# Building the keys and values of both heads of a pair before the attention of either, in a hybrid decoder layer on eight cores

## What is computed

```
q  = (rmsnorm(q_lat) @ w_uq).reshape(B, S, 16, 128 + 64)      # q_lat: 512 wide
kv = (rmsnorm(kv_lat) @ w_ukv).reshape(B, S, 16, 128 + 128)   # kv_lat: 256 wide
q_nope, q_pe = q[..., :128], q[..., 128:]
k_nope, v    = kv[..., :128], kv[..., 128:]
q_pe, k_pe   = apply_rope(q_pe), apply_rope(k_pe)             # k_pe is shared by the heads
s = (q . [k_nope, k_pe]) * 192 ** -0.5, causal
o = softmax(s) @ v
```

## Time and profile before

| | |
|---|---|
| median of 3 runs | 5439.72 us (5438.18 to 5873.62) |
| profiled execution | 5437.82 us, span 5436.2 us (5414.0 to 5436.2 on the cores) |
| PE busy | 4536.3 us, 83% |
| DVE busy | 1777.3 us, 33% |
| ACT busy | 1527.0 us, 28% |
| POOL busy | 208.3 us, 4% |
| mean granted clock of PE, profiled core | 0.921 |

### The profile page before, as it was taken

The page is one execution under the profiler, slowest core; times in us unless marked ns, Lnnn a source line. Parts: engine busy times, 40 slices in busy tenths (PEclk is TensorE's granted clock), DMA queues, the critical chain, the costliest instruction groups (busy, mean ns, idle before and its releaser), DMA issues.

```text
span 5436.2 us, 64110 instructions; the slowest of 8 cores (5414.0 to 5436.2 us)
## 1 busy us (share of the span) xinstructions
PE 4536.3 (83%) x23800; PEld 2196.8 (40%) x23800; DVE 1777.3 (33%) x2983; ACT 1527.0 (28%) x2567; POOL 208.3 (4%) x255
## 2 busy tenths in 40 slices
PE   0657988889966599788889973999999999994995
PEld 0323434444433244344444442444444444443443
DVE  0230015652122311244442115555555555002002
ACT  0441013330113410155451126444444443001001
POOL 1000000000000000000000000000000000110010
PEclk9978999889977799999999985999999999997997
DMA  9626634754455244110114446223232321996996
GB/s 152 124 33 89 93 61 70 115 81 72 77 147 125 35 74 74 33 24 13 19 20 67 75 116 194 50 57 60 51 66 51 66 51 53 219 219 181 218 217 181
DMA packets 354497, 505.64 MB, mean 93 GB/s; under 512 B 9232, under 2 KB 293904, under 8 KB 341648
## 3 DMA queue, kind: packets, MB, share of 16 engines
q0 software_dynamic: 267840, 282.08, 33.3%
q1 hardware_dynamic: 86352, 219.47, 12.7%
HBM read 726.96 MB, written 56.62 MB: 144 GB/s over the span
## 4 chain that ended last, share of the span: by engine, by line
PE 77%; DMA 8%; DVE 7%; ACT 3%; issue 2%; another core or an unknown queue 1%; DVEq 0%; POOL 0%; ACTq 0%; SPq 0%; POOLq 0%
PE ps L1031 22%; PE ps L1079 11%; PE ps L603 4%; PE ps L912 4%; PE ps L631 4%; PE ps L511 4%; PE ps L641 4%; PE ps L947 4%; PE ps L922 4%; DMA out<-sb_scr 3%; PE ps L883 2%; DMA wslot<-w_ada 2%; PE ps L869 2%; PE ps L871 2%; PE ps L885 2%
## 5 line engine op out<-in xcount | busy, mean ns | idle before, releaser
L1031 PE MATMUL ps<-sb_big,wslot 128*128 128x512 bf16 x5632 | 1217.7, 379 | 0.0
L1031 PEld LDWEIGHTS ps<-sb_big,wslot 128*128 128x128 bf16 x5632 | 551.6, 98 | 665.7 <-issue 2.5
L1044 DVE SCALAR_TENSOR_TENSOR sb_scr<-sb_scr,sb_cols 128x512 f32<-128x512 f32 x704 | 529.0, 751 | 469.2 <-ACT sb_scr L1040 431.4
L1079 PE MATMUL ps<-sb_mergedT,wslot 128*128 128x512 bf16 x2816 | 615.5, 382 | 46.2 <-DMA sb_mergedT<-gv_scr 29.2
L1079 PEld LDWEIGHTS ps<-sb_mergedT,wslot 128*128 128x128 bf16 x2816 | 276.5, 98 | 384.9 <-issue 58.4
L1038 ACT ACTIVATE sb_scr<-ps 128x512 f32<-128x512 f32 x352 | 210.2, 597 | 679.4 <-PE ps L1031 482.6
L878 ACT ACTIVATE sb_scr<-ps 128x512 bf16<-128x512 f32 (+3 forms) x640 | 333.8, 533 | 174.7 <-PE ps L871 87.9
L846 DVE RECIPROCAL sb_scr<-ps 128x512 f32<-128x512 f32 x64 | 214.9, 3358 | 389.8 <-PE ps L885 389.8
L1040 ACT ACTIVATE sb_scr<-ps,sb_cols 128x512 f32<-128x512 f32 x352 | 271.8, 772 | 0.0
L869 PE MATMUL ps<-sb_scr 128*128 128x512 bf16 (+3 forms) x640 | 231.0, 361 | 24.3 <-DVE sb_scr L826 21.5
L631 PE MATMUL ps<-sb_big,wslot 128*128 128x512 bf16 x1024 | 233.5, 381 | 16.8 <-DMA wslot<-w_ag 16.8
(11 more groups left out here) (158 smaller groups left out, 4038.5 us busy)
## 6 DMA issues: line engine op xcount, KB each, us to landing
sb_mergedT<-gv_scr SPq DMA_DIRECT2D x88, 1024.0 KB, 6.5
wslot<-w_ada POOLq DMA_DIRECT2D x24, 2048.0 KB, 23.8
wslot<-w_up POOLq DMA_DIRECT2D x22, 2048.0 KB, 14.6
wslot<-w_down POOLq DMA_DIRECT2D x88, 512.0 KB, 8.6
wslot<-w_in POOLq DMA_DIRECT2D x16, 2048.0 KB, 16.2
sb_scr<-x SPq DMA_DIRECT2D x32, 1024.0 KB, 6.7
wslot<-w_ag POOLq DMA_DIRECT2D x16, 2048.0 KB, 14.2
wslot<-w_bg POOLq DMA_DIRECT2D x16, 2048.0 KB, 14.1
```

Source lines behind the costliest of these rows:

```text
L1031: ins = e.matmul(ps[pb][:, :], lhsT=wv[:, kc, c0:c0 + 128], rhs=h2T[:, kc, tsl], start=(kc == 0), stop=(kc == KC - 1))
L1044: P.op("dve", lambda e, hb=hb, yb=yb, ch=ch, tap=tap, off=off: e.scalar_tensor_tensor(out=yb, in0=hb[:, off:off + 512], scalar=cols[:, C_C ...
L1079: ins = e.matmul(ps[oc * 2 + t2][:, :], lhsT=wv[:, f, oc * 128:(oc + 1) * 128], rhs=gslot[sl_][:, f, t2 * 512:(t2 + 1) * 512], start=(g == ...
```

## The change

The K/V projections of both heads are emitted before the score stage of either. For that the second head gets buffers of its own, `KnT_b` and `Vh_b`, with tokens of their own. They are not part of `scr`. The loop over `hd` is split in two, and the tuple `KV` says which buffers a head uses. The numbers of matmuls, copies, loads and bank allocations stay the same, and so does the order of the allocations from `pbank`.

```diff
+    KnT_b = sb("KnT_b", [128, S], BF16)
+    Vh_b = sb("Vh_b", [128, 16, 128], BF16)
...
+    t_KnT_b = P.toks(4)
+    t_Vh_b = P.tok()
+    KV = ((KnT, Vh, t_KnT, t_Vh), (KnT_b, Vh_b, t_KnT_b, t_Vh_b))
...
             for hd in range(2):
-                h = 2 * pr + hd
+                KnT_h, Vh_h, t_KnT_h, t_Vh_h = KV[hd]
                 for kt in range(nk512):
...
-                    P.op("dve", lambda e, pb=pb, ksl=ksl: e.tensor_copy(out=KnT[:, ksl], in_=ps[pb][:, :]),
-                         reads=[t_ps[pb]], writes=[t_KnT[kt]])
+                    P.op("dve", lambda e, pb=pb, ksl=ksl, KnT_h=KnT_h: e.tensor_copy(out=KnT_h[:, ksl], in_=ps[pb][:, :]),
+                         reads=[t_ps[pb]], writes=[t_KnT_h[kt]])
...
-                         reads=[t_ps[pb2]], writes=[t_Vh])
+                         reads=[t_ps[pb2]], writes=[t_Vh_h])
+            for hd in range(2):
+                h = 2 * pr + hd
+                KnT_h, Vh_h, t_KnT_h, t_Vh_h = KV[hd]
                 LOOK = 2
                 pend = []
...
-                    P.op("pe", f, reads=[t_Vh, t_pt[k_], t_ones], writes=[t_ps[po_], t_ps[psm_]])
+                    P.op("pe", f, reads=[t_Vh_h, t_pt[k_], t_ones], writes=[t_ps[po_], t_ps[psm_]])
...
-                            e.matmul(ps[pb][:, c0:512], lhsT=KnT[:, kb * 128:(kb + 1) * 128], rhs=QnT[hd][:, qsl],
+                            e.matmul(ps[pb][:, c0:512], lhsT=KnT_h[:, kb * 128:(kb + 1) * 128], rhs=QnT[hd][:, qsl],
...
-                        P.op("pe", mms, reads=[t_KnT[kb // 4], t_QnT[hd], t_Qr[hd], t_kpe[kb // 4], t_ident, t_mask],
+                        P.op("pe", mms, reads=[t_KnT_h[kb // 4], t_QnT[hd], t_Qr[hd], t_kpe[kb // 4], t_ident, t_mask],
                              writes=[t_ps[pb]])
...
-                            e.matmul(ps[po][:, c0:512], lhsT=Vh[:, kb, :], rhs=ptile[sl_][:, c0:512], start=(kb == 0),
+                            e.matmul(ps[po][:, c0:512], lhsT=Vh_h[:, kb, :], rhs=ptile[sl_][:, c0:512], start=(kb == 0),
                                      stop=(kb == nkb - 1))
```

More of the change, by code:

```diff
@@ L837, in attention @@
                     P.op("pe", mmv, reads=[wt, t_kvg[0][kt], t_kvg[1][kt]], writes=[t_ps[pb2]])
-                    P.op("act", lambda e, pb2=pb2, kt=kt: e.activation(out=Vh[:, 4 * kt:4 * kt + 4, :].rearrange("p k d -> p (k d)"),
+                    P.op("act", lambda e, pb2=pb2, kt=kt, Vh_h=Vh_h: e.activation(out=Vh_h[:, 4 * kt:4 * kt + 4, :].rearrange("p k d -> p (k d)"),
                                                                        in_=ps[pb2][:, :], func=AF.Copy),
-                         reads=[t_ps[pb2]], writes=[t_Vh])
+                         reads=[t_ps[pb2]], writes=[t_Vh_h])
+            for hd in range(2):
+                h = 2 * pr + hd
+                KnT_h, Vh_h, t_KnT_h, t_Vh_h = KV[hd]
                 LOOK = 2
@@ L848, in finalize, with emit_pend @@
                                                           op=ALU.mult), reads=[t_ps[po], t_rec], writes=[t_oT[h][tt]])
-                def emit_pend(ent):
+                def emit_pend(ent, t_Vh_h=t_Vh_h):
                     f, k_, po_, psm_, fin = ent
-                    P.op("pe", f, reads=[t_Vh, t_pt[k_], t_ones], writes=[t_ps[po_], t_ps[psm_]])
+                    P.op("pe", f, reads=[t_Vh_h, t_pt[k_], t_ones], writes=[t_ps[po_], t_ps[psm_]])
                     if fin is not None:
@@ L866, in attention, with mms @@
                         cnt += 1
-                        def mms(e, hd=hd, kb=kb, i=i, c0=c0, qsl=qsl, pb=pb):
-                            e.matmul(ps[pb][:, c0:512], lhsT=KnT[:, kb * 128:(kb + 1) * 128], rhs=QnT[hd][:, qsl],
+                        def mms(e, hd=hd, kb=kb, i=i, c0=c0, qsl=qsl, pb=pb, KnT_h=KnT_h):
+                            e.matmul(ps[pb][:, c0:512], lhsT=KnT_h[:, kb * 128:(kb + 1) * 128], rhs=QnT[hd][:, qsl],
                                      start=True, stop=False)
@@ L880, in attention, with mmo @@
                              reads=[t_ps[pb]], writes=[t_pt[sl_]])
-                        def mmo(e, kb=kb, c0=c0, sl_=sl_, nkb=nkb, po=po, psm=psm):
-                            e.matmul(ps[po][:, c0:512], lhsT=Vh[:, kb, :], rhs=ptile[sl_][:, c0:512], start=(kb == 0),
+                        def mmo(e, kb=kb, c0=c0, sl_=sl_, nkb=nkb, po=po, psm=psm, Vh_h=Vh_h):
+                            e.matmul(ps[po][:, c0:512], lhsT=Vh_h[:, kb, :], rhs=ptile[sl_][:, c0:512], start=(kb == 0),
                                      stop=(kb == nkb - 1))
```

## The result

The changed kernel takes 5350.95 us in the median. Set against runs of the kernel before on the same chips, the ratio is 0.983, with a 95% interval from 0.9816 to 0.9845: 1.7% faster. The cores of the profiled execution need 5312.8 to 5349.3 us, where they needed 5414.0 to 5436.2; their mean falls from 5422 to 5332.

A forecast was written before the change was run, and what follows sets the result against it. TensorE was taken as the bound, with 130 us idle and some low clock in attention. The terms -117.1 + 29.4 + 2.0 - 2.4 + 7.2 + 3.2 - 4.3 - 5.9 + 1.0 gave -86.9 us: 5352, range 5325 to 5400.

The forecast's parts named there:

- the bounds of the sum: Whole kernel with all unknowns at their dear or cheap ends: gain 56 us (time 5383) to 103 us (time 5336).
- within 2%: Whole kernel: time differs from before by no more than 2% (109 us); chance 0.84, against 0.14 faster and 0.02 slower.
- The removed stage: Middle K/V stage between the heads' scores leaves its place: 50.4 us in block 0, 66.8 in block 1, minus 117.1.
- Front, block 1: Before head 0's scores: head 1's K/V matmuls plus 29.4 us, later score start plus 2.0, K cast waits minus 2.4.
- Front, block 0: Before head 0's scores: head 1's K/V matmuls slip into existing waits; scores 0.9 us later per pair, plus 7.2.
- PV wait: Block 0, head 1's second PV half waits 0.4 us per pair for banks 1 and 4: plus 3.2 us.
- Clock in block 0: Score stages in block 0 regain clock as idle PE shrinks: minus 4.3 us for head 1, minus 5.9 for head 0.
- the second rival: Clock comes back whole, with front waits at 0.35 us and no wait of head 1's PV: 5338 us; chance 0.18.
- Loads: Block 0, pair 0: its successor's weights, loaded behind two `w_ada` loads, may land 0 to 2.8 us late; plus 1.0.
- The third rival: Block 0 becomes bound by loads: pairs 0 to 3 wait some 3 us each, 18 us in all, 5370; chance 0.06.
- move to the front: Rival in block 1: four added casts exposed before scores and PE at lower clock, 4.0 us a pair, 5385; chance 0.12.
- many short stops: Rival at head 0's scores: bank stops hold PE near clock 0.71, costing 89 us, 5441 or slower; chance 0.03.

The follow-up runs named there:

- the filling of the front wait: The kernel before, with 10 unused matmuls of 512 columns in front of head 0's scores in each pair of block 0; ratio 0.9977.
- the best kernel: The changed kernel with projection banks restarted at each pair as 2, 3, 5, 6, 7, 1, 4 and Q copies on ACT; 5297 us, mean over cores 5279.

## Why the prediction was right, and where it failed

**The time.** 5352 was forecast and 5351 measured, and the walk through the queues behind it holds nearly row by row. The step that failed is the last one, "Two per cent, about what a measurement of this kernel can tell from no change". The runs showed an interval of a seventh of a per cent to each side, so a gain of 1.7% is eleven times clear of no change. By that bound 0.84 was given to "within 2%" for a case whose own rows said faster in every branch but one: the bounds of the sum ended at 56 us of gain. The chances should have said that the kernel gets faster, and how sure that was. Two terms of the sum behind the time were mis-sized as well, the clock in block 0 and the loads, and hit it only together (below).

**The removed stage** (-117.1) is gone, with the idle time that hung on it.

**Front, block 1** (plus 29.4, 2.0 and minus 2.4). About 8.5 us from the first K matmul to the first score was stated. The front stages now take, in stretches of PE:

```profile
2400.31:2408.66 8.35, 7.18 (x81) 1.00 0.00 0
...
sum 66.03, PE 58.13; mean PE 7.27
```

Eight last 66.0 us, 8.3 each, with another 2.7 us of score waits in all. Block 1 gained 42.7 where the terms give 37.8. Part of the 4.9 us between them is in the Q stages (2.3 by my reading of the trace), where PE is busy for 2.4 us less; I had left them as they were.

**Front, block 0** (plus 7.2): the extra wait is 0.8 a pair by my reading of the trace, instead of 0.9. "About 4.5" for the stage was a slip of mine, since 1.9 + 2.2 + 0.9 is 5.0, and 5.1 is measured. **PV wait** (plus 3.2): 2.2 measured (L891 behind L855, eight times 0.3), so the place was right.

**Clock in block 0** (minus 10.2) was mis-sized: 20.7 us of busy time came back, of which 14.1 reached the length of the score stages, with the PV wait already in it; the two terms together had 7.0. I took half of head 0's loss because a shorter stop stayed. Every one of the eight pairs now has 1.00, and the filling of the front wait showed that all of head 0's loss hung on that one wait. What I had as the second rival is in this term the truth. I had also left out that PE at full clock waits more for ACT.

**Loads** (plus 1.0) were mis-sized the other way: 9.3 us on core 7, 7.9 on core 5, 4.8 on the mean. I read the landing time of 24.9 on the profiled core, in pair 3; in pairs 0 to 2 of that core the second block took 26.4, 25.6 and 26.7. On core 3 of the same execution the one of pair 0 took 34.5 us, which I hadn't looked at:

```profile
wslot<-w_ada POOLq DMA_DIRECT2D x1, 2048.0 KB, 34.5
```

The third rival, loads as bound, is thus true for pair 0 alone and small for the others. The clock is wrong by some 7 us one way and the loads by 8.3 on core 7 the other way, so they cancel on the slowest core. The 4.9 us more of block 1 are met by as much scatter outside attention: the stages lose 91.7 us from core 5 to core 7, the spans 86.9. That the sum (-86.9) equals the last number is luck; on the mean of the cores the stages gain 95. Of the signs stated, idle PE fell by 54 us where 60 to 75 were named, and the clock in block 0 is 0.94 where 0.91 to 0.93 was: less from idle time, more from the clock. The waits at the change of pair, whose growth would have proved the prediction wrong, did not grow (20.9 us against 20.7 in block 1).

**Rivals.** The wait didn't move to the front in block 1: no stage there exceeds 8.6 us. The wait at the meeting of the heads is gone. PE isn't slowed by many short stops: the projections have V waits of 1.2 us at most, and the clock behind them is 1.00. The Trainium skill, "TensorE: Matmul & The Clock Gate", "A second HAM failure mode: psum-queue depth-cycling", describes a PE that cycles through PSUM banks and stops so often between groups of matmuls that its clock swings. This trace doesn't bear that out: all 16 front stages, with twice the projections in a row, have 1.00.

**What stays open.** On core 5 the middle stages of three pairs in block 1 kept a clock of 1.00 behind idle times of 2.8 to 3.2 us, while others of 3.2 to 4.5 lost it. The length of the stop alone doesn't decide: on core 7 of the same execution the same 3.17 us gave 0.84 and 0.88 in two of those three pairs. Why is open. That the loads of all cores compete in pair 0 is argued from the spread between cores, and wasn't tried.

## What to carry to other kernels

Where an engine with an in-order queue idles at a seam, ask first which lock it stands at (here banks that a slow reciprocal still reads), and then which lock stands behind that (the queue of the engine that empties the banks); curing one gives its full worth only with the other. A second buffer is worth what it lets move: left in place it gave nothing, with the stage moved 95 us. Moving the stage was not the only cure: other banks and copies on ACT gave 112 us in the old order (5421.5 to 5310), and the best kernel, which has the new order as well, 145 (5424 to 5279). And look at the slowest core of each load before a transfer is called hidden, since the next stage may come to it on any core.

## What the runs showed of the hardware

- Idle stretches of 2.2 to 4.5 us cost TensorE another third to three quarters of their length through its clock (core 5): 13.9 us of busy time behind 19.1 us of waits in block 0 (head 0), 9.4 behind 28.1 in block 1. Filled with useless matmuls the same stages run at 1.00, and with the filling in block 1 the kernel with more work is the faster one (ratio 0.9976).
- In one execution of the kernel before, the same second load of 2 MB took 26.4 us to land on core 5 and 34.5 on core 3; one with nothing ahead of it took 14.5 on core 5.
- With its idle time nearly gone (best kernel) PE ran the 485 us of attention of block 1 at a granted clock of 1.00, on all eight cores.
